# A two-layer decoder step: eight column groups instead of four run with K outermost during the conditioning, and the rates follow as 32 small steps

## The reference, cut to what matters

```python
c_act = jax.nn.silu(c)
mod = (c_act @ w_ada[0] + b_ada[0])          # 9 rows of c, w_ada is 2048 x 12288
sh1, sc1, g1, sh2, sc2, g2 = split_cols(mod, [2048] * 6)
h = rms_norm(x, norm_mix[0]) * (1.0 + sc1) + sh1
z = h @ ev_w_in[0]                           # 2048 x 4112
q, k, v, r, a_lr, u = split_cols(z, [512, 512, 1024, 1024, 16, 1024])
# gated linear attention over q, k, v with decays from a_lr; causal pooling of u;
# both then go through ev_w_out; x = x + g1 * y, and the MLP with sh2, sc2, g2
```

## Time and profile before

| | |
|---|---|
| median of 3 runs | 2581.65 us (2581.54 to 2583.17) |
| profiled execution, span from its first to its last instruction | 2583.8 us |
| TensorE busy in it | 2534.5 us (98%) |
| LDWEIGHTS busy | 2445.3 us (95%) |
| DVE, ACT, GpSimd busy | 1505.9, 979.2, 149.2 us |
| mean granted TensorE clock | 0.991 |
| moved by DMA | 616.56 MB, mean 239 GB/s |

### The profile page before, as it was taken

One profiled execution on the slowest core, in us unless ns is written; L12 is line 12 of the kernel. 1 busy time (PEld: TensorE's weight loads), 2 busy tenths in 40 slices (PEclk: granted clock), 3 DMA queues, 4 the chain that ended last, 5 costly groups with the idle time before them and its releaser, 6 DMA issues.

```text
span 2583.8 us, 59693 instructions
## 1 busy us (share of the span) xinstructions
PE 2534.5 (98%) x25197; PEld 2445.3 (95%) x25197; DVE 1505.9 (58%) x2253; ACT 979.2 (38%) x1105; POOL 149.2 (6%) x195
## 2 busy tenths in 40 slices
PE   7899999999999999999999999999999999999998
PEld 5788789999999999999999999999999999999998
DVE  3465455555455445445548987987655554655554
ACT  2143253333233233233335555456433333333333
POOL 1000241100000000000020010100000000000011
PEclk8899999999999999999999999999999999999999
DMA  9988979799899899988655454655555555555553
GB/s 353 364 318 285 309 273 323 262 325 315 296 309 314 301 303 306 309 301 302 226 179 170 157 185 162 193 159 165 165 178 179 179 178 180 178 178 178 179 178 131
DMA packets 476310, 616.56 MB, mean 239 GB/s; under 512 B 10535, under 2 KB 379525, under 8 KB 471785
## 3 DMA queue, kind: packets, MB, share of 16 engines
q1 hardware_dynamic: 469458, 591.70, 69.1%
q0 software_dynamic: 6720, 22.96, 2.8%
HBM read 602.77 MB, written 13.26 MB: 238 GB/s over the span
## 4 chain that ended last, share of the span: by engine, by line
PE 89%; DVE 4%; DMA 4%; ACT 2%; issue 1%; POOL 0%; SPq 0%; ACTq 0%; DVEq 0%; POOLq 0%
PE ps L921 26%; PE ps L922 25%; PE ps L923 25%; PE pm L1043 5%; DMA wide<-in_w_ada 3%; PE ps L965 1%; PE pm L1022 1%; DVE w_lo L2062 1%; PE pm L1055 1%; PE pm L1205 1%; ACT w_hi L1538 1%; DVE z L2632 0%; DMA st<-in_state_gla 0%; PE pm L1285 0%; PE ps L1114 0%
## 5 line engine op out<-in xcount | busy, mean ns | idle before, releaser
L2062 DVE TENSOR_TENSOR w_lo<-raw,w_hi 128x1024 fp32r<-128x1024 f32 x708 | 878.5, 1242 | 866.5 <-ACT w_hi L1538 860.6
L1538 ACT ACTIVATE w_hi<-raw 128x1024 fp32r<-128x1024 f32 x696 | 735.3, 1058 | 1236.8 <-PE ps L923 1214.2
L921 PE MATMUL ps<-h_hi,w_hi 128*128 128x264 f32 x3616 | 1049.2, 290 | 5.3 <-DVE h_lo L2487 3.2
L922 PE MATMUL ps<-h_lo,w_hi 128*128 128x264 f32 x3616 | 1032.2, 285 | 0.0
L923 PE MATMUL ps<-h_hi,w_lo 128*128 128x264 f32 x3616 | 1030.8, 285 | 0.0
L921 PEld LDWEIGHTS ps<-h_hi,w_hi 128*128 128x128 f32 x3616 | 684.7, 189 | 25.7 <-issue 17.6
L922 PEld LDWEIGHTS ps<-h_lo,w_hi 128*128 128x128 f32 x3616 | 683.2, 189 | 0.7
L923 PEld LDWEIGHTS ps<-h_hi,w_lo 128*128 128x128 f32 x3616 | 683.0, 189 | 0.0
L921 PE MATMUL ps<-f_hi,w_hi 128*128 128x264 f32 x2048 | 585.5, 286 | 0.0
L922 PE MATMUL ps<-f_lo,w_hi 128*128 128x264 f32 x2048 | 583.9, 285 | 0.0
L923 PE MATMUL ps<-f_hi,w_lo 128*128 128x264 f32 x2048 | 583.2, 285 | 0.0
(11 more groups left out here) (379 smaller groups left out, 1633.3 us busy)
## 6 DMA issues: line engine op xcount, KB each, us to landing
raw<-in_mlp_w_up SPq DMA_DIRECT2D x128, 1024.0 KB, 6.0
raw<-in_mlp_w_down SPq DMA_DIRECT2D x128, 1024.0 KB, 5.4
wide<-in_w_ada SPq DMA_DIRECT2D x104, 1024.0 KB, 9.6
wide_late<-in_w_ada SPq DMA_DIRECT2D x56, 1024.0 KB, 9.6
raw<-in_od_w_in SPq DMA_DIRECT2D x48, 1024.0 KB, 5.2
raw<-in_ev_w_in SPq DMA_DIRECT2D x32, 1024.0 KB, 7.3
araw<-in_w_ada SPq DMA_DIRECT2D x24, 1024.0 KB, 9.7
raw<-in_ev_w_out SPq DMA_DIRECT2D x16, 1024.0 KB, 5.4
```

The costliest lines, as they stand in the source:

```text
L921: nc.tensor.matmul(acc, w_hi[:, slot, cols], xh[:, k, :], start=(k == UK * ends[0]), stop=False)
L922: nc.tensor.matmul(acc, w_hi[:, slot, cols], xl[:, k, :], start=False, stop=False)
L1538: nc.scalar.activation(w_hi[:, u, :], raw[:, p, u, :], ACT.Copy).then_inc(hi_ready, 1)
L2062: nc.vector.tensor_tensor(w_lo[:, p, u, :], raw[:, p, u, :], w_hi[:, u, :].bitcast(F32), ALU.subtract).then_inc(lo_ready, 1)
```

## The change

**Early part.** Eight groups (EARLY = 8) run with K outermost, so each quarter has 8 units and their sums go to z in 8 steps. SyncE loads rows of 1024 columns more; the order of loads around a pair of wides is: wide 2q+2, two halves of quarter q (groups 4 to 7), wide 2q+3, two halves of quarter q+1 (groups 0 to 3). TensorE's order becomes units 0 to 3, wide 2q+2, units 4 to 6, wide 2q+3, unit 7. Wide 0 is now taken chunk by chunk between the first transposes. The squares of x are summed by three ACT instructions over the rows of x, and two matmuls with a diagonal replace the 32.

**After it.** 36 units remain with something beside them: units 4 to 7 of quarter 3 (side units 0 to 3) and groups 8 to 15 (side units 4 to 35). The rates are 32 steps of one K tile, with two buffers, at side units 0 to 15 and 17 to 32. `ada_rows` (DVE) and `ada_turn` (TensorE) are both in side unit 16, and 33; `ada_add` is in 17, and 34. The mixer's 48 steps are paced: two steps at side units 0 to 7, 12, 13, 28 and 29, one at the others. GpSimd loads the first two sample states when 8 groups are out of PSUM.

The core of the diff:

```diff
-PAIR_STEPS = 8
-ADA_STEPS = 2 * PAIR_STEPS
+EARLY = 8
+SIDE_UNITS = 4 + 4 * 8
+ADA_STEPS = 2 * KT
+def ada_step(unit):
+    if unit < KT:
+        return unit
+    return unit - 1 if KT < unit <= 2 * KT else None
+
+DOUBLED = (0, 1, 2, 3, 4, 5, 6, 7, 12, 13, 28, 29)
+PACE = [2 if unit in DOUBLED else 1 for unit in range(SIDE_UNITS)]
...
 @block.sync
+            def rates0(n):
+                if n < 2:
+                    sp.wait_ge(wide_used, 4 * (WIDES - 1) + n + 1)
+                else:
+                    sp.wait_ge(ada_used, n - 1)
+                col = ADA_RATES[n // KT] * P
+                sp.dma_start(araw[:, n % 2, :, :], ada[0][:, n % KT:n % KT + 1, col:col + D]...).then_inc(ada_in[n % 2], 16)
...
+            def early(q, j, h):
+                n = 2 * q + j
+                if n >= 2:
+                    sp.wait_ge(split_used, NU * (n - 2) + (2 * h + 2))
+                col = (2 * j + h) * WIDE
+                sp.dma_start(half_rows(raw, j, h), w[:, UK * q:UK * q + UK, col:col + WIDE]).then_inc(raw_in[j][h], 16)
+
+            wide(0)
+            early(0, 0, 0)
+            wide(1)
+            early(0, 0, 1)
+            for q in range(QUARTERS - 1):
+                wide(2 * q + 2)
+                early(q, 1, 0)
+                early(q, 1, 1)
+                wide(2 * q + 3)
+                early(q + 1, 0, 0)
+                early(q + 1, 0, 1)
+            early(3, 1, 0)
+            early(3, 1, 1)
...
+            rates0(0)
+            rates0(1)
+            late_group(8, 0)
+            late_group(8, 1)
+            rates0(2)
+            for i in range(9, 16):
+                n = 4 * (i - 9) + 3
+                late_group(i, 0)
+                rates0(n)
+                rates0(n + 1)
+                late_group(i, 1)
+                rates0(n + 2)
+                rates0(n + 3)
...
 @block.gpsimd
-                    pool.wait_ge(ada_used, 2 * PAIR_STEPS)
+                    pool.wait_ge(evacuated, EARLY)
...
 @block.tensor
+            def token_squares():
+                pe.wait_ge(diag_ready, 1)
+                nc.tensor.matmul(pm[:, 0, 0:TP], ones[:, :], diag[:, 0:TP], start=True, stop=True)
+                nc.tensor.matmul(pm[:, 0, TP:T], ones[0:NS, :], diag[0:NS, TP:T], start=True, stop=True,
+                                 skip_group_check=True).then_inc(ss_done, 8)
...
             for q in range(QUARTERS - 1):
-                for h in range(2):
-                    w = 2 * q + 2 + h
-                    wide_half(w, 0)
-                    wide_half(w, 1)
-                    quarter_products(q, 2 * h)
-                    wide_turn(w)
-                    quarter_products(q, 2 * h + 1)
+                w = 2 * q + 2
+                for v in range(4):
+                    quarter_products(q, v)
+                wide_half(w, 0)
+                wide_half(w, 1)
+                quarter_products(q, 4)
+                wide_turn(w)
+                quarter_products(q, 5)
+                quarter_products(q, 6)
+                wide_half(w + 1, 0)
+                wide_half(w + 1, 1)
+                quarter_products(q, 7)
+                wide_turn(w + 1)
                 gate_rows(q)
...
-            for i in range(4, 16):
-                def beside(u):
-                    if u == 1:
-                        ada_group(2 * i - 7 if i < 8 else i)
-                    if u == 2 and i in (7, 15):
-                        ada_turn(i // 8)
+            def beside0(unit):
+                n = ada_step(unit)
+                if n is not None:
+                    ada_row(n)
+                elif unit in (KT, 2 * KT + 1):
+                    ada_turn(unit // KT - 1)
+                for _ in range(PACE[unit]):
                     next(mixer, None)
+            for v in range(4, EARLY):
+                quarter_products(3, v)
+                beside0(v - 4)
+            for i in range(EARLY, 16):
+                products(i, i % 2, h_hi, h_lo, h_wait(0), lambda u: beside0(NU * (i - EARLY) + u + 4))
...
 @block.vector
             for q in range(QUARTERS - 1):
                 w = 2 * q + 2
+                evac_quarter(q, 0)
+                evac_quarter(q, 1)
+                evac_quarter(q, 2)
+                lo_quarter(q, 4)
+                lo_quarter(q, 5)
+                evac_quarter(q, 3)
+                wide_copy(w)
+                lo_quarter(q, 6)
+                lo_quarter(q, 7)
+                evac_quarter(q, 4)
+                wide_add(w, wide_at(w))
+                scale_quarter(q + 1)
+                evac_quarter(q, 5)
+                evac_quarter(q, 6)
+                wide_copy(w + 1)
+                lo_quarter(q + 1, 0)
+                evac_quarter(q, 7)
+                wide_add(w + 1, wide_at(w + 1))
+                shift_quarter(q + 1)
+                for v in range(1, 4):
+                    lo_quarter(q + 1, v)
...
+            for unit in range(SIDE_UNITS):
+                i, u = EARLY + unit // NU, unit % NU
+                if i == EARLY:
+                    evac_quarter(3, u + 4)
+                lo(i, u, i % 2)
+                if unit in (KT, 2 * KT + 1):
+                    ada_rows(unit // KT - 1)
+                if unit in (KT + 1, 2 * KT + 2):
+                    ada_add(unit // KT - 1)
+                for _ in range(PACE[unit]):
                     next(mixer, None)
```

More of the change, by code:

```diff
@@ L304, in build @@
         mod_ready = sem("mod_ready")
-        ada_in = [sem(f"ada_in{h}") for h in range(4)]
+        ada_in = [sem(f"ada_in{h}") for h in range(2)]
         wide_in = [sem(f"wide_in{i}") for i in range(4)]
@@ L326, in build @@
         sq_ready = sem("sq_ready")
+        diag_ready = sem("diag_ready")
         ss_done = sem("ss_done")
@@ L492, in transfers @@
             return before + b // HEADS[q]["bufs"] + 1
[L494 to L510, removed]
         def half_rows(t, p, h):
@@ L1008, in gemm, with ada_row @@
                 one(count - 1, 1, None if w0 is None else w0 + (count // 2 - 1), earlier_squares)
-            def ada_group(a):
-                if a == 0:
+            def ada_row(n):
+                if n == 0:
                     pe.wait_ge(wide_rows, WIDES)
-                elif a == PAIR_STEPS:
+                elif n == KT:
                     pe.wait_ge(mod_ready, 1)
[L1017 to L1024, removed]
+                pe.wait_ge(ada_in[n % 2], 16 * (n // 2 + 1))
+                k = n % KT
+                for q in range(QUARTERS):
+                    last = nc.tensor.matmul(pm[q * CP:(q + 1) * CP, 3, :], c_pad[:, k, :], araw[:, n % 2, q, :],
+                                            start=(k == 0), stop=(k == KT - 1), tile_position=(0, q * CP))
+                last.then_inc(ada_used, 1)
             def ada_turn(b):
@@ L1031, in ada_turn, with wide_chunk @@
                 last.then_inc(turned, 1)
+            def wide_chunk(w, c, chunks=wides):
+                pe.wait_ge(wide_in[c], 16 * (w + 1))
+                for i in range(4):
+                    k = 4 * c + i
+                    for q in range(QUARTERS):
+                        last = nc.tensor.matmul(pm[q * CP:(q + 1) * CP, 3, 0:P], c_pad[:, k, :], chunks[c][:, i, q * P:(q + 1) * P],
+                                                start=(k == 0), stop=(k == KT - 1), tile_position=(0, q * CP))
+                last.then_inc(wide_used, 1)
             def wide_half(w, half, chunks=wides):
-                if half == 0 and not (isinstance(w, int) and w == 0):
+                if half == 0:
                     pe.wait_ge(wide_rows, w)
[L1038 to L1042, removed]
-                            last = nc.tensor.matmul(pm[q * CP:(q + 1) * CP, 3, 0:P], c_pad[:, k, :], chunks[c][:, i, q * P:(q + 1) * P],
-                                                    start=(k == 0), stop=(k == KT - 1), tile_position=(0, q * CP))
-                    last.then_inc(wide_used, 1)
+                wide_chunk(w, 2 * half, chunks)
+                wide_chunk(w, 2 * half + 1, chunks)
             def wide_turn(w):
```

171 lines of the change are left out of this document (64 added, 107 removed).

## The result

| | before | changed |
|---|---|---|
| median | 2583.17 us (5 runs, 2581.54 to 2584.72) | 2591.98 us (5 runs, 2590.80 to 2594.99) |
| ratio | | 1.0034, interval [1.0022, 1.0046] |
| profiled execution, span | 2583.8 us | 2590.1 us |
| mean granted TensorE clock | 0.991 | 0.996 |

The change made the kernel 8.8 us slower (0.34%). The forecast was 2577.0, range 2564 to 2589: wrong sign, and 3 us outside the range.

A forecast was written before the change was run, and what follows sets the result against it. It took DMA to bound the early part and TensorE nearly all the rest; 8.3 - 35.0 + 2.4 + 10.0 + 7.9 - 1.8 + 3.6 = -4.6 from 2581.65 gave 2577.0 us, range 2564 to 2589.

The forecast's parts named there:

- E: End of the last product standing alone, before rates and recurrence: from 151.3 to 159.6 us, +8.3, bounds +5 to +17.
- the early part isn't filled: Rival, 11%: before E each quarter loses 3 us more, 9 in all, as splits, sums and h share DVE: 2586.
- Start: Early part: wide 1 is used up by 41.0 instead of 43.7, so TensorE begins its products at about 43.5 us.
- 12 units fewer, -35.0: After E: 36 units instead of 48 remain, each 2.92 us: -35.0 us.
- Rate steps, 1.0 each: After E: 32 one-tile rate steps of 1.0 us against 16 of 1.85: +2.4 us (0 to +10).
- The recurrence, +10.0: Side units 0 to 7: at double pace TensorE waits at each set, and set 1 comes late: +10.0 us, bounds 5 and 14.
- The ring: Recurrence: ACT's split, DVE's split, prefix, factors and difference, ACT's exponentials, then ACT's next split: 5.85 us per level.
- Hand-offs, +7.9: Units 16, 17, 33: TensorE waits 3.0, 2.6 and 3.0 us for rates behind the splits: +7.9 us (0 to 8.6).
- States and DMA, -1.8: Side units 15 to 23: DMA up to 7.2 us per unit against TensorE's 5.7; waits 3.2 again: -1.8 us (-5 to +9).
- The slower rival on states: Rival, 16%: DMA becomes the bound among the sample states, state loads landing later: 2587.7 us.
- The clock, +3.6: Two low-clock spells of 1.8 us each, behind units 17 and 33: +3.6 us (0 to +20).
- the clock falls in the recurrence: Rival, 6%: at 1.2 GHz a unit takes 8.7 us, 2.9 more for seven units: 2597 us.

The follow-up runs named there:

- the rates ahead: Changed kernel with DVE copying and adding the rates ahead of its own split in side units 16, 17, 33 and 34: 2584.44 us, ratio 1.0003.
- The two pace edits: Double steps moved: units 0, 2, 4, 6, 8-13 on the changed kernel, 2591.25 us; units 2, 3, 5, 6, 8-13 with rates ahead of splits, 2581.93.
- the later chunks: Changed kernel with each chunk of wide 0 one group of transposes later at start-up: 2593.40 us, ratio 1.0042; four further kernels include this edit.

## Why the prediction was wrong

**The failed step: "E becomes 159.6: +8.3 us".** E came at 169.4, +18.1. In the step's own terms the 9.8 us between are:

| term | forecast | measured | more |
|---|---|---|---|
| first product | 43.5 | 46.9 | 3.4 |
| from there until wide 3 is used up | 28.8 | 30.2 | 1.4 |
| two quarters, wide to wide | 33.1 each | 34.9 and 35.2 | 3.9 |
| wait behind wide 7 | 5.3 | 6.2 | 0.9 |
| from the last first product to E | 15.8 | 16.0 | 0.2 |

The step within it that failed is the sentence "a quarter is 33.1 us against 32.6 for its 12 loads, almost balanced". Of the 5.3 that it holds for the wait, unit 7 and the gate's matmuls are 4.4, so it gave TensorE 32.2 us of work and 0.9 of idle time. Measured were 33.2 of work and 1.5 and 2.1 of idle time. The way from a wide to h was 6.2 instead of 5.3, and TensorE's own work alone is as long as the whole forecast. I had compared the sum with DMA's 32.6 as if the larger of two nearly equal numbers were the result; with both that close, the waits came on top.

A balance would have warned. Before, TensorE was busy 91.0 us between 43.7 and 151.3, at a clock of 0.87. Twelve units of 2.92 are 35.0 more: 126.0 us, less what a full clock gives back, at most 14.0 (0.13 of 107.6). So E could lie between 155.7 and 169.7 without a single wait. The forecast, 159.6, stood in the lower third of that, and its lower bound of +5 (156.3) lay within 1 us of that floor. The busy time turned out to be 117.1 us, some 116 at full clock (an estimate: less 1% of 122.5).

The rival held at 11%, "the early part isn't filled", was the case that came: its 9 us more put E at 168.6. That the number fits is partly luck. Its 3 us per quarter were 1.8 and 2.1 in the two middle quarters, and the start brought the rest.

**From the span to the median.** The forecast took 2.15 us off for the difference between the median shown and the profiled span. The changed kernel's profiled execution took 2591.98 in all, 1.9 more than its span, so the profiled execution of before was one of its slower ones (2583.8 and 1.9 is more than any of its five runs), and measured from it the base was some 4 us low. With 9.8 of E and 1.4 behind it this is the whole 15.0, within 0.3.

**Start.** "TensorE can begin its products at about 43.5" took h's delay from the earlier trace rows and the earlier landing from DMA. Eleven profiles with two orders of start-up began between 43.9 and 46.9. The three in which TensorE was busy all of the 20 us from 20 to 40 began at 45.2 to 46.9, the others, which waited for chunks there, at 43.9 to 45.2. The forecast's "a stretch whose end is set by wide 1's landing" holds for the latter only. The bounds should have held both.

**12 units fewer, -35.0.** No stage holds this term alone; a unit measured 2.9 (169.40 to 172.28) to 3.0 (11.92 for four, 83.38 to 95.30), against the 2.92 taken.

**Rate steps, 1.0 each.** Right: 1.00 in the chain, the view from which the 1.85 for two was read. (The timeline, which counts the last matmul to its end, has 1.06 and 1.92 for the same.)

**The recurrence, +10.0.** The ring was read right (5.8), and its whole price is the idle time of the first stage, 8.0. Its parts, 4.9 ahead of set 1 and 5.2 behind, were 4.1 and 3.9 (with 0.7 of another wait). What the term left out is the low clock behind the wait ahead of set 1, 1.7 us here and 3.4 with the rates ahead. The two pace edits bear it out: one shortens the stage by 1.3 to 1.9, by the second part, the other by 4.3 to 4.8, by both and the clock.

**Hand-offs, +7.9.** The best term: 9.2 in the stages, 7.5 in the medians when taken away (clock included). They were real, they weren't hidden by DMA, and four moved lines undo them.

**States and DMA, -1.8.** Idle time from the 17th to the 32nd rate step was 2.1 us, loads' waits 2.1 in all, against 3.2 before: -1.1. The slower rival on states did not come; in the six kernels without the hand-offs' idle time the waits for araw and states were 2.2 to 6.2 us, so a part of a repair can be lost there.

**The clock, +3.6.** Behind E before, 0.01 of 245.6 us, 2.5; after, by the four stages (0.02, 0, 0.04 and 0.05 of them), 7.1: +4.6. The forecast had two spells of 1.8 us, behind units 17 and 33. There were three: 1.7 behind the wait ahead of set 1, which had been given nothing, 3.4 behind unit 17 and 1.7 behind unit 33 (0.95 and 0.88 in the two windows from 367 to 387 us). With the hand-offs taken away the stages behind them had 0.98 and 1.00 instead of 0.96 and 0.95.

The rival "the clock falls in the recurrence" did not come as it was priced: the stage has 0.98, and from 190 to 200 us, with the ring's gaps of 0.3 to 1.0 us between sets, 1.00. It came as one spell behind the wait of 4.1 us. The Trainium skill, "TensorE: Matmul & The Clock Gate", section on HAM oscillation, tells of a kernel whose waits for data are longer than the work between them, so that each burst starts at the low clock, while with work much longer than the waits the clock stays up. The trace agrees for the ring, where the 5.8 us of a level hold gaps of at most about 1 us.

So the second part was forecast within 1.4 us by terms that each hold within 2, part of it by errors of opposite sign (recurrence 2.0 too much, hand-offs 1.3 too little), and 9.8 us of the miss in the trace are in the first part, where the quarter's sum was compared with DMA's and never with TensorE's own work.

## What to carry to other kernels

When work is moved into a gap, first make a balance: the engine's busy time there plus what is moved in, from the start that a trace has shown; the end can't be earlier than that, less what a higher clock gives back, and with a second resource as full as this one the waits came on top (33.2 us of work and 32.6 of loads made quarters of 34.8 and 35.2). Where three engines hand a value round within a program order, put what the next engine waits for ahead of what it doesn't: four moved lines on DVE were worth 7.5 of the 8.8 us that the change had lost. And a chain names who came last, not what it would be worth to help it: the 14.1 us load stood 0.7 us ahead of the next in line.

## What was not expected of the hardware

- From the first product to 60 us TensorE is busy throughout in all eleven kernels, and yet the granted clock there is 0.84 to 0.90 in the six with the changed kernel's start-up and 0.79 to 0.85 in the five with the later chunks. What sets it isn't shown.
- Three waits, of 4.1, 3.1 and 2.6 us, were each dearer than their idle time in some profile. The clock fell towards half speed right behind them, which cost 1.7 us (0.67 over 5 us) to 3.4 us (0.55 and 0.77 over 10 us). The waits in units 16 and 17 had one such spell in the changed kernel, behind the second wait, and in the four other kernels that keep them it came behind the first; so the stage took 16.3 us or 18.9 to 19.4 for the same idle time of 5.7, and what looked cheap had moved into the next stage. Without the waits it was 10.6 in all six.
